# The key and value projection of a two-layer decode step, made of seven block products per pair of column tiles instead of eight

## The reference

```python
def shared_kv(x, g_kv, w_kv):
    kv = (rms_norm(x, g_kv) @ w_kv).reshape(B, T, 2 * N_BRANCH, N_KV, HEAD_DIM)
    return [kv[:, :, i] for i in range(2 * N_BRANCH)]   # k_cmp, v_cmp, k_slc, v_slc, k_win, v_win

def rms_norm(x, g):
    y = xf * lax.rsqrt(jnp.mean(xf * xf, axis=-1, keepdims=True) + RMS_EPS)
    return y * g
```

## Time and profile before

| what | value |
|---|---|
| runs without profile | 2425.74, 2426.16, 2420.20 us; median 2425.74 |
| profiled execution, span | 2418.8 us |
| median less span | 6.9 us |
| TensorE busy | 2353.9 us, 97% |
| VectorE busy | 1179.0 us, 49% |
| ScalarE busy | 824.5 us, 34% |
| GpSimd busy | 356.3 us, 15% |
| DMA | 419.69 MB, mean 174 GB/s |

### The profile page before, as it was taken

How to read it: one execution, slowest core, us unless ns; L and a number is a source line. 1 busy time by engine, 2 the same in 40 slices (tenths; PEclk the granted TensorE clock), 3 DMA queues, 4 the chain that set the end, 5 groups by cost and what they waited for, 6 DMA issues and landing times.

```text
span 2418.8 us, 48921 instructions
## 1 busy us (share of the span) xinstructions
PE 2353.9 (97%) x20326; PEld 2219.0 (92%) x20326; DVE 1179.0 (49%) x2056; ACT 824.5 (34%) x1383; POOL 356.3 (15%) x517
## 2 busy tenths in 40 slices
PE   7999999999999999999989999999999999998997
PEld 6988888888899999999979999999989988867997
DVE  1236111221163344333577777777666666654343
ACT  1125211111242232111344444444455545543222
POOL 2002000592000000110220000000033323313000
PEclk9999999999999999999999999999999999999998
DMA  9986887667644435773444444444533333498222
GB/s 342 350 295 190 262 261 240 196 223 228 214 139 142 132 105 193 235 236 106 140 83 131 131 131 131 131 131 132 153 105 105 105 92 96 152 334 301 88 88 89
DMA packets 401174, 419.69 MB, mean 174 GB/s; under 512 B 21991, under 2 KB 354023, under 8 KB 398579
## 3 DMA queue, kind: packets, MB, share of 16 engines
q1 hardware_dynamic: 384610, 349.70, 46.4%
q0 software_dynamic: 16368, 67.15, 8.3%
HBM read 383.59 MB, written 55.27 MB: 181 GB/s over the span
## 4 chain that ended last, share of the span: by engine, by line
PE 92%; DVE 3%; ACT 1%; DMA 1%; issue 1%; POOL 0%; SPq 0%; ACTq 0%; DVEq 0%; POOLq 0%
PE acc L2469 43%; PE acc L2620 19%; PE acc L2647 8%; PE work L2384 4%; PE work L2673 3%; PE work L2324 3%; PE out_acc L2710 2%; PE work L2739 1%; PE acc L2324 1%; PE acc L2695 1%; PE work L2372 1%; PE acc L2752 1%; PE out_acc L2705 1%; PE work L2664 1%; DMA block<-in_w_in_b 1%
## 5 line engine op out<-in xcount | busy, mean ns | idle before, releaser
L2469 PE MATMUL acc<-h_hi,w_hi 128*128 128x260 f32 x2832 | 581.7, 287 | 2.5 <-DVE w_lo L1574 1.9
L1574 DVE TENSOR_TENSOR w_lo<-raw,w_hi 128x1024 fp32r<-128x1024 f32 (+1 forms) x220 | 272.0, 1237 | 624.2 <-ACT w_hi L1146 624.0
L2469 PE MATMUL acc<-h_hi,w_lo 128*128 128x260 f32 x2832 | 571.1, 283 | 0.0
L2469 PE MATMUL acc<-h_lo,w_hi 128*128 128x260 f32 x2832 | 570.4, 283 | 0.0
L1146 ACT ACTIVATE w_hi<-raw 128x1024 fp32r<-128x1024 f32 (+1 forms) x220 | 231.0, 1051 | 783.9 <-PE acc L2469 774.9
L2469 PEld LDWEIGHTS acc<-h_hi,w_hi 128*128 128x128 f32 x2832 | 436.2, 189 | 29.0 <-issue 27.6
L2469 PEld LDWEIGHTS acc<-h_hi,w_lo 128*128 128x128 f32 x2832 | 437.5, 189 | 0.0
L2469 PEld LDWEIGHTS acc<-h_lo,w_hi 128*128 128x128 f32 x2832 | 437.0, 189 | 0.0
L1907 DVE TENSOR_TENSOR block_lo<-block,block_hi 128x1024 fp32r<-128x1024 f32 x168 | 205.4, 1224 | 111.2 <-ACT block_hi L1387 110.9
L1387 ACT ACTIVATE block_hi<-block 128x1024 fp32r<-128x1024 f32 x168 | 177.6, 1058 | 200.1 <-DVE block L1942 64.5
L2620 PE MATMUL acc<-t_hi,block_hi 128*128 128x260 f32 x768 | 217.3, 283 | 2.7 <-DVE block_lo L1907 2.1
(11 more groups left out here) (412 smaller groups left out, 3498.4 us busy)
## 6 DMA issues: line engine op xcount, KB each, us to landing
ada<-in_w_ada SPq DMA_DIRECT2D x192, 512.0 KB, 4.9
block<-in_w_in_b SPq DMA_DIRECT2D x96, 512.0 KB, 4.6
raw<-in_w_in_a SPq DMA_DIRECT2D x64, 512.0 KB, 4.9
raw<-in_w_kv SPq DMA_DIRECT2D x48, 512.0 KB, 3.6
raw<-in_w_out_a SPq DMA_DIRECT2D x32, 512.0 KB, 3.8
raw<-in_w_in_b SPq DMA_DIRECT2D x32, 512.0 KB, 4.4
raw<-in_w_out_b SPq DMA_DIRECT2D x32, 512.0 KB, 3.5
pages_early<-in_cache_k_cmp SPq DMA_DIRECT2D x32, 256.0 KB, 4.3
```

The costliest lines, as they stand in the source:

```text
L1574: V.tensor_tensor(LO[j % 2][:, :, 0:n], RAW[j][:, :, 0:n], HI[j % 2][:, :, 0:n].bitcast(F32), ALU.subtract).then_inc(lo_ready, 1)
L2469: last = mm_(out[half][0:n, 0:HT], part[slot][:, kk, cols_], src[:, k, half * HT:(half + 1) * HT], start=(first and part is HI and src is ...
```

## The change

Q_KV is made by the seven products too, 12 pairs x 7 products. Block column 0 or 1 of the features is now the even or the odd tiles ("(k c p) n -> c p k n"), so that the activations of B11, B12 come from even rows of X and B21, B22 from odd rows. The operands are made in pieces during Q_OA, as rows of X become final: ScalarE writes X times the gain into XGE (even) and XGO (odd), and splits b11; GpSimd makes the row sums T3 and T1 for rows 0 to 6, later T2 and T4 over several rows in place; the last row (7) is made by VectorE after Q_OA's end. T1, T2, T4 and T3 are split when they exist, and take the places of X, HH, HL and Y as these come free, so X is written out in four pieces during Q_OA and read back in four pieces at the end of Q_KV. The order of the six results is v_slc, v_win, k_slc, k_win, k_cmp, v_cmp (KV_ORDER). The token copies of the first 25 turns move from VectorE to ScalarE, with two buffers instead of four; GpSimd's b_scr copies move a little earlier. The last pair's P2 and P3 are added up inside `apply(1)`, the last five turns stand between the two hidden products, and the activation of hidden(16) stands at row 10 of `apply(1)`. The later stages only count their semaphores from other numbers. The diff, cut to its core:

```diff
+Q_U, Q_Z, Q_MIX, Q_OA, Q_KV, Q_G, Q_P, Q_H, Q_OB = 0, 8, 16, 18, 26, 47, 48, 90, 98
+K_0 = 4 * Q_KV
+K_PAIR = 12
+K_LAST = K_0 + (K_PAIR - 1) * N_PROD
+KV_ORDER = (3, 5, 2, 4, 0, 1)
+KV_TURN = {(0, 1): 0, (0, 3): 1, (0, 5): 2, (1, 0): 3, (1, 1): 4}
+OPERANDS = ("b11", "t1", "t2", "t4", "t3", "b21", "b22")
...
@@ SyncE @@
-            quads(Q_KV, w_kv, 12)
+            def kv_load(q, role, c, m):
+                at = (2 * KV_ORDER[q // 2] + q % 2) * 256 + P * m
+                src = w_kv.rearrange("(k c p) n -> c p k n", c=2, p=P)[c]
+                sp.dma_start(RB[role][:, :, :], src[:, :, at:at + P]).then_inc(raw_full[role], 16)
...
+                if q:
+                    sp.wait_ge(lo_ready, K_0 + N_PROD * (q - 1) + S_P7 + 1)
+                    kv_load(q, R_A11, 0, 0)
...
@@ GpSimd @@
+            for i in range(1, 8):
+                r = i - 1
+                pool.wait_ge(xg_ready, 2 * r + 2)
+                pool.wait_ge(kp_ready, LO_PARTS[f"b11_{r}"])
+                nc.gpsimd.tensor_tensor(T3F[:, r, :], XGO[:, r, HT:T], XGE[:, r, HT:T], ALU.subtract)
+                nc.gpsimd.tensor_tensor(XGE[:, r, 0:HT], XGE[:, r, HT:T], XGE[:, r, 0:HT], ALU.subtract).then_inc(kt_ready, 1)
...
+                if i >= 5:
+                    pool.wait_ge(kp_ready, LO_PARTS[f"t1_{i - 5}"])
+                    t_sum(*((0, 4), (4, 5), (5, 7))[i - 5], 1).then_inc(kt_ready, 1)
+            pool.wait_ge(kp_ready, LO_PARTS["t2_0"])
+            t_sum(0, 7, -1).then_inc(kt_ready, 1)
...
-            pool.wait_ge(h_ready, 2 * KT)
-            pool.dma_start(x_scr, flat(X[:, :, :])).then_inc(s_xs, 16)
+            for c in range(4):
+
+                pool.wait_ge(w_used, K_LAST + (S_P5, S_P5, S_P2, S_P3)[c] + 1)
+                pool.dma_start(flat(X[:, 4 * c:4 * c + 4, :]), x_scr[:, 4 * c * T:4 * (c + 1) * T]).then_inc(s_x1[c], 16)
 
             pool.wait_ge(amod, 2)
-            pool.wait_ge(s_xs, 16)
             apply(1)
@@ ScalarE @@
+            for i in range(8):
+                hi(Q_OA + i, 1)
+                if i:
+                    squares(1, i - 1)
+                    x_gain(2 * i - 2)
+                    x_gain(2 * i - 1)
+                    b11_hi(i - 1)
+                hi(Q_OA + i, 2)
+                if i in (5, 6, 7):
+                    t1_hi(i - 5)
+                if i == 7:
+                    b21_hi(0)
+                    t2_hi(0)
+                hi(Q_OA + i, 3)
+                if i < 7:
+                    hi(Q_OA + i + 1, 0)
+            t4_hi(0)
+            t3_hi(0)
+            kv_hi(0)
+            x_gain(14)
+            b11_hi(7)
+            kv_hi(1)
+            t1_hi(3)
+            x_gain(15)
+            t2_hi(1)
+            kv_hi(2)
+            t4_hi(1)
...
+            for p in range(N_PROD * K_PAIR):
+                q, s = divmod(p, N_PROD)
+                if s in (S_P1, S_P5):
+                    act.wait_ge(w_used, K_0 + p + 1)
+                    wait(act, st_added, 9 * (q - 1) + (5, 6)[s])
+                    nc.scalar.activation((K1C, K5C)[s][:, :], D[s][:, 0:HT], ACT.Copy).then_inc(st_copied, 1)
+                if p + 3 < N_PROD * K_PAIR:
+                    kv_hi(p + 3)
+                if p == 0:
+                    squares(1, 7)
+                    t3_hi(1)
+                    b21_hi(1)
+                elif p == 1:
+                    act.wait_ge(w_used, K_0)
+                    part_hi("b22", XGO, 0, 8)
+                elif p == 2:
+                    rms(1)
...
@@ VectorE @@
                     if a == 0 and k == KT + 1:
                         compress_out(15)
-                    if a == 1 and k == 2:
-                        lo(Q_G - 1, 3)
-                    if a == 1 and k == 7:
-                        kv_out(5, 1, VF)
+                    if a == 1 and k == 1:
+                        kv_step(K_PAIR - 1, S_P2)
+                    if a == 1 and k == 4:
+                        kv_step(K_PAIR - 1, S_P3)
+                    if a == 1 and k == 9:
                         for n in range(25, 29):
                             token_rows(n)
...
+            def beside(i):
+
+                def step(j):
+                    if i and j == 1:
+                        b11_lo(i - 1)
+                    elif i in (5, 6, 7) and j == 2:
+                        t1_lo(i - 5)
+                    elif i == 7 and j == 3:
+                        part_lo("t2", XGE, 0, 7, "t2_0")
+                    elif i == 7 and j == 0:
+                        part_lo("t4", XGE, 0, 7, "t4_0")
+                        kv_s1(0)
+                        part_lo("t3", T3F, 0, 7, "t3_0")
+                        kv_lo(0)
+                return step
+
+            for i in range(8):
+                turn_a(i, beside(i))
+            b11_lo(7)
+            last_row_sum(1)
+            t1_lo(3)
+            kv_lo(1)
+            last_row_sum(2)
+            last_row_sum(3)
+            part_lo("t2", XGE, 7, 8, "t2_1")
+            kv_s2(0)
+            kv_lo(2)
+            last_row_sum(4)
+            part_lo("t4", XGE, 7, 8, "t4_1")
+            kv_lo(3)
+            part_lo("t3", T3F, 7, 8, "t3_1")
+            kv_s3(0)
+            kv_step(0, S_P6)
+            kv_lo(4)
             square_sum(1, 7)
+            dve.wait_ge(w_used, K_0)
+            part_lo("b21", XGO, 0, 8, "b21_1")
+            dve.wait_ge(s_x0, 64 + 64)
+            part_lo("b22", XGO, 0, 8, "b22_0")
+            for p in range(2, N_PROD * K_PAIR):
+                q, s = divmod(p, N_PROD)
+                if p > 2 and s in (S_P6, S_P7, S_P2, S_P3) and p < N_PROD * K_PAIR - 2:
+                    kv_step(q, s)
+                if s == S_P3 and q + 1 < K_PAIR:
+                    kv_s3(q + 1)
+                if p + 3 < N_PROD * K_PAIR:
+                    kv_lo(p + 3)
+                    ahead_q, r = divmod(p + 3, N_PROD)
+                    if r == S_P5:
+                        kv_s2(ahead_q)
+                    elif r == S_P2:
+                        kv_s4(ahead_q)
+                    elif r == S_P1:
+                        kv_s1(ahead_q)
...
+                elif s == S_P7:
+                    dve.wait_ge(st_copied, 2 * q + 2)
+                    V.tensor_tensor(K1C[:, :], D[3][:, 0:HT], K1C[:, :], ALU.add).then_inc(st_added, 1)
+                    dve.wait_ge(st_added, 9 * q + 2)
+                    V.tensor_tensor(K5C[:, :], K5C[:, :], K1C[:, :], ALU.add).then_inc(st_added, 1)
+                    V.tensor_tensor(K1C[:, :], K1C[:, :], D[2][:, 0:HT], ALU.subtract).then_inc(st_added, 1)
+                    if q == 0:
+                        rstd(1)
...
@@ TensorE @@
+                out = D[(0, 1, 3, 2, 3, 0, 1)[s]]
+                b_hi, b_lo = KHI[OPERANDS[s]], KLO[OPERANDS[s]]
+                begin = s in (S_P1, S_P5, S_P6, S_P4)
+                for kk in range(8):
+                    for part, w, b in ((0, HB, b_hi), (1, HB, b_lo), (2, LB, b_hi)):
+                        last = mm_(out[:, 0:HT], w[slot_of(p)][:, kk, :], b[:, kk, :],
+                                   start=(begin and kk == 0 and part == 0), stop=(kk == 7 and part == 2), skip_group_check=True)
+                last.then_inc(w_used, 1)
+
+            for q in range(K_PAIR):
+                for s in range(N_PROD):
+                    kv_product(q, s)
+                    if q == 0 and s == S_P4:
                         stat(1)
+                    if q >= 2 and (q % 2, s) in KV_TURN:
+                        kv_turn(5 * (q // 2 - 1) + KV_TURN[q % 2, s])
...
+            pe.wait_ge(s_cwp[0], 64)
+            hidden(16, 0, KVF[0], W1P)
             for n in range(25, 30):
                 kv_turn(n)
-            pe.wait_ge(s_cwp[0], 64)
-            hidden(16, 0, KCF, W1P)
             pe.wait_ge(s_cwp[1], 64)
-            hidden(17, 1, VCF, W1P, True, 3)
+            hidden(17, 1, KVF[1], W1P, True, 3)
```

More of the change, by code:

```diff
@@ L345, in build @@
+        TML = [place(f"last_token_rows{i}", [P, 512]) for i in range(5)]
+        CSILP = [place(f"c_hidden_prompt{i}", [P, NKV * NCMP]) for i in range(2)]
         assert cursor[0] <= x_at
+        cursor[0] = keep_end - TS * NKV * NCMP * 4
+        TM = [place(f"token_rows{i}", [P, 512]) for i in range(2)]
+        assert cursor[0] <= c_top
+        spot = 8 * HT * 4
+        at_h = lambda n: h_at + n * spot
+        at_l = lambda n: y_at - 4 * spot + n * spot
+        at_y = lambda n: y_at + n * spot
@@ L536, in build @@
         s_pooled_s = sem("pooled_samples_ready")
-        s_x0 = sem("x_first_out")
-        s_x1 = [sem(f"x_first_back{i}") for i in range(4)]
+        s_x0 = sem("x_spilled")
+        s_x1 = [sem(f"x_back{i}") for i in range(4)]
         s_ph = sem("pooled_hi_ready")
@@ L1236, in apply @@
                         hi(Q_U, {5: 0, 9: 1, 13: 2}[k])
-                    if a == 1 and k == 2:
-                        hi(Q_G - 1, 3)
+                    if a == 1 and k == 10:
+                        hidden(16, 0, CSILP)
             act.wait_ge(amod, 1)
@@ L1723, in body @@
```

(3 more changed lines are left out.)

541 lines of the change are left out of this document (340 added, 201 removed).

## The result

The changed kernel takes **2443.36 us** (median of four runs, 2442.78 to 2445.11) against 2423.65 for the kernel before (four, 2420.20 to 2426.16): ratio 1.0083, 95% interval 1.0071 to 1.0096. It is slower by 20 us; 2421 was forecast. The profiled execution has a span of 2443.4 us, 24.6 more than before.

The account below looks back on a forecast made before the run. TensorE, busy 97% of the span, bounds the kernel. Products -34.6, start +21.4, end +7.7 and steady state +1 sum to -4.5 us: span 2414.3, time 2421, range 2407 to 2435.

Parts of the forecast that it names:

- Products: Q_KV stage: 2016 matmuls instead of 2304, 288 fewer at 0.120 us, all on the path, 34.6 us saved.
- steady state: Q_KV's pairs: VectorE's work mostly fits in 20.2 us a pair; 1 us lost in all, bounds 0 and 4.
- Rival 4: Q_KV products: no gain per product, one-bank products with waits at 0.134 us a matmul; +20, 2450 us; chance 0.03.
- Start: Q_OA's end to the second pair: P1 at 8.2 us, second pair at 45.9; 21.4 us more lost, bounds 15 and 26.
- VectorE goes on without a pause: Start of Q_KV, after P1 starts: VectorE's low parts follow each other without gaps, P5's at 10.6 us, P4's at 18.5.
- Middle: Q_KV between start and end: 2.88 us a product and no wait on weight blocks.
- rival 2: Q_KV: weight blocks, A11 of the next pair, land after 9.7 us of slack; +11.6, 2437 us; chance 0.15.
- End: Last product to the gates' first quad: 30.4 us instead of 22.7, 7.7 us lost, bounds 5 and 12.
- The pieces need 5.3 us each and are in time: End of Q_KV: X's four 1.04 MB pieces are read back in time, the first three issued before the last product ends.
- The sum: Whole kernel: -34.6 + 21.4 + 7.7 + 1 = -4.5; span 2414.3, time 2421, with runs' median 6.9 above span.
- Rest: OA's loop, X's spill, b_scr copies and small compress weights: nothing lost; spill and b_scr copies bounded at 0 and 1.
- What would show it: Signs; refuted by a start gap under 4 us, ScalarE block waits in the middle, or time under 2412 or over 2432.

Follow-up runs that it names:

- experiment 5: Changed kernel, start laid anew (T4 on VectorE, B21's low part on GpSimd, more): 2441.2 us; second version, B21 back on VectorE, copies in Q_OA: 2427.9 us.
- the last kernel: Changed kernel with start and end laid anew, 11 window-state copies placed one per pair after the next block's landing, five in Q_OA: 2417.0 us, 0.9985.

## Why the prediction was wrong

**Products: right.** 288 fewer matmuls at 0.12 us. Without the copies in the way the 77 products from the second pair on, with 25 turns, took 237.8 us; 77 x 2.88 + 25 x 0.44 + 2.3 for the low clock at their start is 235.1. That leaves 2.7 us of steady state against the 1 taken, inside its bounds of 0 to 4. Rival 4 is dead: where nothing waits, 48 matmuls of the stage take 5.74 to 5.79 us, 0.120 each. (Its 0.134 us a matmul would have eaten 28 of the 34.6; all of it needs 0.137.)

**Start: right in kind, 2.5 us too low.** Forecast: P1 at 8.2, a wait ahead of the square sum, 4.9 idle behind the reciprocal, the second pair at 40.65 us. Measured: 9.6, 2.2, 4.8 and 43.2, the clock at 0.50 from 915 to 920. T4 on GpSimd took 4.10 us, where I took 3.5: 0.6 of the 2.5 us. It also began 0.4 us late. What is left fits hand-overs, which the sum had only in its upper bound: "VectorE goes on without a pause" was wrong, since from 919 to 953 us it stands eight times for a high part of ScalarE's, 5.6 us in all. The estimate from the Trainium skill ("GPSIMD Engine Reference", section 3.1) had been 4.0 us for T4, so here the page was nearer than my choice among the rows. VectorE stood idle for 5.97 us around T4; what moving it alone would give, no run tells, since experiment 5 moves other instructions with it. GpSimd's and VectorE's timelines of the changed kernel, answering to the earlier trace rows:

```profile
904.63 4.10 POOL L1064 TENSOR_TENSOR x_gain_even<-x_gain_even,x_gain_odd 128x1820 f32<-128x1820 f32 x1 [6.01 <-DVE kv_t_lo L2035]
```

```profile
910.52 2.06 DVE L2035 TENSOR_TENSOR kv_t_lo<-x_gain_even,kv_t_hi 128x1820 fp32r<-128x1820 f32 x1 [5.97 <-ACT kv_t_hi L1447]
```

**Middle: the step that failed.** The sum put the waits for weight blocks at nothing. The reasons were "Against: the DMA share in such a stretch is 0.78 at most" and "five copies now fall in 40.4 us", and rival 2 got a chance of 0.15. The runs showed 15.8 us above the forecast in this stretch (252.2 against 236.4), 14.5 of them the copies' in the traces. The mechanism was described as it came: A11 of the next pair lands too late beside the copies (9.6, 11.3, 10.4 and 11.5 us in the chain) and the products wait. Three sizes were off.

- The copies go by the turns of token rows, and the code puts five turns into eight products, 23 us and not 40.
- The 0.78 was the share of the old stage at the old pace; where the five copies fall, the new one had 0.88.
- The slack of A11 was 8.2 us and not 9.7. The forecast counted the high and the low part of the block. But what P1 waits for is a row of results that frees its bank, and in VectorE's queue this row stands behind the low part and S1, 1.5 us more. Behind the landing of 11.3 us (at 1019.3), VectorE, then TensorE:

```profile
1020.41 1.22 DVE L2063 TENSOR_TENSOR block_lo<-block,block_hi 128x1024 fp32r<-128x1024 f32 x1 [3.69 <-ACT block_hi L1500]
1021.55 1.22 DVE L2073 TENSOR_TENSOR block<-block,block 128x1024 f32<-128x1024 f32 x1
1022.69 0.42 DVE L2099 TENSOR_TENSOR kv_T<-acc,rstd 128x260 f32<-128x260 f32 x1
```

```profile
1023.25 0.36 PE L2895 MATMUL acc<-kv_b_hi,block_hi 128*128 128x260 f32 x1 [3.05 <-DVE kv_T L2099]
```

Landings of 11.3, 10.4 and 11.5 us left TensorE idle for 3.05, 2.21 and 3.31: 8.2 us of slack each time. The landing of 9.6 cost 0.52; two turns (0.9 us) stood between the products there.

That the rival's price of 16 us was near the 14.5 is in part luck. It took 2.3 us of waiting in each of seven pairs. The trace has three waits over 2 us, one pair in two, and a third of the cost is the low clock behind them, which the price left out. The chance was the error: a load with a bounded slack and a rival transfer of known length should have been laid out in time, as I did with VectorE's instructions, and not weighed by a mean.

**End: 13.6 us and not 7.7.** The delay of GpSimd's rows behind X's last piece came as forecast: its first 8-column product at E + 1.0, VectorE's third norm at E + 1.6 and 14 norms after E. What was left out: SyncE's weight tiles and the read-back of X fall together. 4.2 MB of each are asked for between 1189 and 1215 us, and 8.4 MB at the 341 GB/s of that window are 25 us. "The pieces need 5.3 us each and are in time" took the time of a piece without company; here it was 8.6, and VectorE waited once for a piece, 2.0 us; a compression tile needed up to 14.0. TensorE waited 8.7 us for them, and through the token rows in VectorE's queue the norm waited too. The edits of the end together gave back 3.8 us (36.3 to 32.5 in the last kernel); what each of them gave isn't shown. Of the remaining 2.1 us over the forecast no run tells how they divide between hand-overs and token rows.

**The sum.** In spans the forecast was 29 us too low (2414.3 against 2443.4), in times 22 (2421 against 2443.4). The difference is luck. The 6.9 us carried from span to time were the launch and the spread of three runs: in every later run the launch adds 1.6 to 1.9 us to its span (2445.11 against 2443.4), and the kernel before has medians of 2420.8 to 2422.7. With 1.8 the forecast would have been 2416.

**Rest.** OA's loop hid its new instructions, as said: in the changed kernel Q_OA has 1542 matmuls in 185 us, the same as before.

**What would show it** was well chosen: ScalarE's waits for a block in the middle and a time above 2432 were named as what would refute it, and both came.

## What to carry to other kernels

When a stage is shortened by cutting products, list its transfers against the clock as closely as its instructions: which load has the least slack, what else is issued in those microseconds, and in what bunches. A bulk copy that nothing waits for is free only where it doesn't meet that load; issue it on the landing of the tightest one. Count the slack to what frees the next product, through every queue on the way, and not to the load's own last instruction. And a saving bought with preparation (here 34.6 us of products for 24 us of start and 14 of end) has little room for one more cost: the best version here gains 3.8 us (2420.8 to 2417.0).

## What the runs showed of the hardware

- Beside a two-input subtraction over 2080 columns on GpSimd (5.92 us), VectorE's subtraction over 260 columns, started behind it, took 4.83 us instead of 0.43; the one that VectorE had started before it kept its 2.05.
- Weight blocks of 512 KB landed in a median of 5.3 us in 512 B runs beside the 1 MB copies, in 4.1 us in 4 KB runs beside the same copies, and in 4.4 us in 512 B runs without the copies.
- From 1195 to 1215 us the DMAs moved 341 GB/s at a share of 0.99; a 512 KB tile then took up to 14.0 us.
- After waits of TensorE of 3.05 and 3.31 us the granted clock of the next 8 and 9 us was 0.79 and 0.67; after one of 2.21 us it was 1.00.
- The runs spread more with all copies in Q_OA (12.9 us over 12 runs, 2413.5 to 2426.3) than with 11 of them placed in the stage (5.2 us over 11 runs, 2415.1 to 2420.4), on different chips. Why, stays open.
